# Weights' buffers at four places within 256 bytes, in a two-block sequence model on one core

## The reference

```python
h = rms_norm(x, norm_g)
parts = jnp.split(h @ w_in, split_idx, axis=-1)
...
return x + mixed @ w_out
```

## Time and profile before

| what | value |
|---|---|
| time, median of 3 runs | 3272.28 us (3271.72 to 3272.84) |
| the profiled execution | 3274.4 us |
| its span, first to last instruction | 3272.6 us |
| mean granted TensorE clock | 0.998 of 2.4 GHz |
| instructions | 43,047 |
| matmuls | 15,826, of them 12,672 in the units |

### The profile page before, as it was taken

The page is one execution under the profiler, slowest core; times in us unless marked ns, Lnnn a source line. Parts: engine busy times, 40 slices in busy tenths (PEclk is TensorE's granted clock), DMA queues, the critical chain, the costliest instruction groups (busy, mean ns, idle before and its releaser), DMA issues.

```text
span 3272.6 us, 43047 instructions
## 1 busy us (share of the span) xinstructions
PE 3250.9 (99%) x15826; PEld 2643.6 (81%) x15826; DVE 2089.6 (64%) x3172; ACT 1268.8 (39%) x1987; POOL 141.8 (4%) x116
## 2 busy tenths in 40 slices
PE   8999999999999999999999999999999999999999
PEld 7888888787888888888878887787778888778777
DVE  5665656687776566534264776677757477676863
ACT  4333324445443345523132224524534222642641
POOL 3000000001020000000020000000002000000000
PEclk9999999999999999999999999999999999999999
DMA  5333436677776676746453454545547354555445
GB/s 178 123 124 109 136 125 196 213 247 264 253 277 203 196 223 191 249 174 212 148 179 106 148 171 148 187 146 177 186 170 255 109 171 132 188 166 180 172 163 203
DMA packets 302097, 588.83 MB, mean 180 GB/s; under 512 B 64280, under 2 KB 111128, under 8 KB 301888
## 3 DMA queue, kind: packets, MB, share of 16 engines
q1 hardware_dynamic: 301888, 586.09, 53.7%
HBM read 453.77 MB, written 132.20 MB: 179 GB/s over the span
## 4 chain that ended last, share of the span: by engine, by line
PE 93%; DVE 3%; ACT 1%; DVEq 1%; DMA 1%; issue 1%; SPq 0%; ACTq 0%
PE bank L561 70%; PE bank L560 13%; PE bank L2007 1%; PE bank L1102 1%; PE bank L738 1%; PE bank L1132 1%; PE bank L1422 1%; PE bank L1453 1%; PE bank L1608 0%; PE bank L1597 0%; PE bank L2328 0%; DVEq L2638 0%; PE bank L1007 0%; PE bank L1610 0%; PE bank L2358 0%
## 5 line engine op out<-in xcount | busy, mean ns | idle before, releaser
L561 PE MATMUL bank<-act_high,weights_high 128*128 128x512 f32 x3584 | 1424.7, 398 | 14.7 <-DVE act_low L544 11.3
L561 PE MATMUL bank<-act_low,weights_high 128*128 128x512 f32 x3584 | 1401.6, 391 | 0.0
L473 DVE TENSOR_TENSOR weights_low<-weights_raw,weights_high 128x1024 fp32r<-128x1024 f32 x528 | 654.4, 1240 | 724.5 <-ACT weights_high L404 711.2
L404 ACT ACTIVATE weights_high<-weights_raw 128x1024 fp32r<-128x1024 f32 x528 | 557.5, 1057 | 1416.3 <-PE bank L561 1206.8
L561 PE MATMUL bank<-act_high,weights_low 128*128 128x512 f32 x3584 | 963.0, 389 | 0.0
L561 PEld LDWEIGHTS bank<-act_high,weights_high 128*128 128x128 f32 x3584 | 676.1, 189 | 163.8 <-DVE act_low L544 11.3
L561 PEld LDWEIGHTS bank<-act_low,weights_high 128*128 128x128 f32 x3584 | 676.2, 189 | 136.2 <-issue 1.2
L561 PEld LDWEIGHTS bank<-act_high,weights_low 128*128 128x128 f32 x3584 | 672.7, 188 | 140.1
L560 PE MATMUL bank<-weights_high,act_high 128*128 128x512 f32 x640 | 253.1, 396 | 0.0
L560 PE MATMUL bank<-weights_high,act_low 128*128 128x512 f32 x640 | 249.4, 390 | 0.0
L2105 DVE SCALAR_TENSOR_TENSOR residual_in<-residual_in,arena 128x512 f32<-128x512 f32 x240 | 181.2, 755 | 20.3 <-issue 1.5
(11 more groups left out here) (323 smaller groups left out, 2484.2 us busy)
## 6 DMA issues: line engine op xcount, KB each, us to landing
weights_raw<-in_w_all SPq DMA_DIRECT2D x528, 512.0 KB, 3.5
convert_in<-mix SPq DMA_DIRECT2D x80, 256.0 KB, 4.4
fm_b<-stream_out SPq DMA_DIRECT2D x72, 256.0 KB, 3.3
mix<-arena SPq DMA_DIRECT2D x64, 256.0 KB, 3.1
x_part<-stream_out SPq DMA_DIRECT2D x48, 256.0 KB, 4.4
residual_in<-x_part SPq DMA_DIRECT2D x48, 256.0 KB, 5.4
x<-stream_out SPq DMA_DIRECT2D x48, 256.0 KB, 5.2
convert_in<-x SPq DMA_DIRECT2D x48, 256.0 KB, 4.0
```

Of the source, the lines that this page charges most:

```text
L404: e.activation(WH[:, t % 3, :], RAW[:, t % 3, :], ACT.Copy).then_inc(wh_ready, 1)
L473: e.tensor_tensor(WL[:, t % 3, :], RAW[:, t % 3, :], WH[:, t % 3, :].bitcast(F32), ALU.subtract).then_inc(wl_ready, 1)
L561: return e.matmul(bank[s][:, :], a[:, s * P:(s + 1) * P], h, start=start, stop=stop)
```

## The change

The three positions of weights_high and weights_low are cut from tensors that have 64 columns more, at columns 16, 1056 and 2096, and 0, 1040 and 2080. In bytes, within 256 and counted from the activations' place, the positions of weights_high lie at 64, 128 and 192, those of weights_low at 0, 64 and 128. The arena gets 128 columns less, and everything declared between weights_low and the arena's end moves by 512 bytes, weights_low itself by 256.

```diff
-        WH = sb("weights_high", [P, 3, 2 * L], F32R)
-        WL = sb("weights_low", [P, 3, 2 * L], F32R)
+        WH_ALL = sb("weights_high", [P, 6 * L + 64], F32R)
+        WL_ALL = sb("weights_low", [P, 6 * L + 64], F32R)
+        WH = [WH_ALL[:, at:at + 2 * L] for at in (16, 1056, 2096)]
+        WL = [WL_ALL[:, at:at + 2 * L] for at in (0, 1040, 2080)]
...
-        ARENA_N = 20032
+        ARENA_N = 19904
...
-            e.activation(WH[:, t % 3, :], RAW[:, t % 3, :], ACT.Copy).then_inc(wh_ready, 1)
+            e.activation(WH[t % 3], RAW[:, t % 3, :], ACT.Copy).then_inc(wh_ready, 1)
...
-            e.tensor_tensor(WL[:, t % 3, :], RAW[:, t % 3, :], WH[:, t % 3, :].bitcast(F32), ALU.subtract
+            e.tensor_tensor(WL[t % 3], RAW[:, t % 3, :], WH[t % 3].bitcast(F32), ALU.subtract
                             ).then_inc(wl_ready, 1)
...
-                a = (WL if part == 2 else WH)[:, b, k * L:(k + 1) * L]
+                a = (WL if part == 2 else WH)[b][:, k * L:(k + 1) * L]
```

## The result

The changed kernel takes 3327.63 us in the median (3326.27 to 3328.73, 5 runs) against 3272.28 for the kernel before: a ratio of 1.0169, with a 95% interval of 1.0158 to 1.0180. It is slower by 55 us. The range of the prediction (3215 to 3360) holds it. The forecast itself, no change, did not come; the loss that the first rival priced did, in a milder form than its full price.

A forecast was written before the change was run, and what follows sets the result against it. TensorE's matmul spacing was taken to bound the kernel. Writers, shifted memory, displaced products and settling were each taken as 0, sum 0, so the forecast stayed at 3272.3 us, range 3215 to 3360.

The forecast's parts named there:

- Rival 1: Displaced products lose their rhythm as load and stream pieces meet: 7.7 ns each, +87 us, 3359 us; slower had chance 0.34.
- line 738's price: Upper price per displaced product, from line 738's 234.4 ns against 226.7: 7.7 ns, x 11,264 = +87 us.
- What bounds the kernel: TensorE, busy 3250.9 of 3272.6 us; the start-to-start spacing of 12,672 matmuls, 226.7 ns each, makes 88% of the span.
- the extra 13.3 ns: Time per matmul over the 213.3 ns of 512 columns at 2.4 GHz; 169 us in all, which buffer places could change.
- the small group that has 7.7 more: Line 738: 32 matmuls of the same shape, stationary operand displaced by 96 bytes, 234.4 ns each instead of 226.7.
- the settling: Matmul runs settle into 226.7 ns; settling anew in each unit was priced at most 28 us, taken as 0.
- Writers, slices, moved tensors, 512 bytes: ScalarE and VectorE writing displaced buffers, and the 512-byte shift of what follows in memory, each cost 0.
- The products: 11,264 products with displaced weights in lines 561 and 560: between -150 and +87 us, taken as 0.
- The reading of line 738: Its operand, displaced by one and a half 64-byte pieces, cuts a ninth piece per load and finds no steady rhythm.
- Its case of 3326 us: Products displaced by 64 and 192 bytes lose the rhythm, those by 128 keep it: +54 us.
- Rival 2: Loads of displaced weights no longer meet the stream: -75 us for one piece, -150 for both; faster had chance 0.22.
- The rule of the Trainium skill: Loading the next weights takes no SBUF read bandwidth from the running matmul, so place means nothing and time is 3272 us.

The follow-up runs named there:

- run 1: Changed kernel, but all positions of both weight parts back at the activations' place within 256 bytes, one period on; 3272.30 us, ratio 1.0003.
- run 3: Kernel before, with padding so that only small_weights, line 738's operand, moves to the activations' place within 256 bytes; 3272.18 us.
- run 4: Changed kernel, with each position's low part at its high part's place (64, 128, 192 bytes past the activations'); 3322.88 us, ratio 1.0155.
- run 5: Changed kernel, with both parts of all positions at 192 bytes past the activations' place; 3300.71 us, ratio 1.0090.
- run 9: Kernel before, places unchanged, each matmul of the units split into two of 256 columns with a weight load each; 3421.34 us.
- run 10: Changed kernel with its four places, each matmul of the units split into two of 256 columns with a load each; 3352.09 us.
- run 11: Against the kernel before: all weights at 64 bytes past the activations' place, 256-column halves only where weights are stationary; 3301.60 us, ratio 1.0086.
- run 12: Against the kernel before: stationary weights at 64 bytes with 256-column halves, moving weights whole at place 0; 3293.07 us, ratio 1.0068.

## Why the prediction was right, and where it failed

The range held because it took in line 738's price; the forecast at its centre missed by 55 us, where the prediction had said that 6.5 us can be told.

- **What bounds the kernel**: right. The extra 13.3 ns, the small group that has 7.7 more, and the settling were the rows that mattered, and line 738 was shown to be a matter of place.
- **Writers, slices, moved tensors, 512 bytes**: right; run 1 prices them all together at nothing, 1.0003.
- **The products**: this is the step that failed. "I take 0" rested on 64 bytes being the unit, with 96 bad only because it is no multiple of 64. The measured spacing at 64, 128 and 192 is 233.2, 232.4 and 229.1 ns; the period is 256 bytes as far as tried (run 1), and of the thirteen places only 0 runs at 226.7 throughout, and that where all weights lie there. Of the two known rows, line 738's was the nearer one after all.
- **The reading of line 738** that carried this step was wrong as well, and the trace of the kernel before had the answer. It was said not to settle in 32 matmuls. Its first start is at 64.55 us; from there, every seventh is:

```profile
66.19 0.39 PE L738 MATMUL bank<-act_low,small_weights 128*128 128x512 f32 x1
...
67.83 0.39 PE L738 MATMUL bank<-act_high,small_weights 128*128 128x512 f32 x1
...
69.47 0.39 PE L738 MATMUL bank<-act_low,small_weights 128*128 128x512 f32 x1
...
71.11 0.39 PE L738 MATMUL bank<-act_high,small_weights 128*128 128x512 f32 x1
```

They are 1.64 us apart, four times over. The group is settled, in a longer cycle: 238, 237, 231, 234, 235, 234, 231 ns, the same to 1 ns in all three groups, and 1.64 us are 246 pieces of 6.67 ns. The commonest cycles at the other places tried here are whole numbers of pieces too: 34 in one step at 0, 35 at 64 (or 70 in two), 103 in three at 192, 244 in seven at 128; with halves, 18 in one at 0 and 17 in one or 53 in three at 64. So that a rhythm counts in whole pieces does not tell a good place from a bad one.

- **Rival 1** has the sign and the order of what happened; its mechanism, pieces that meet, no run shows. Its price per displaced product, 7.7 ns, was an upper bound as named: the mean over all products rose by 4.8 ns, from +3 at 192 to +6 at 64 with stationary weights. Its case of 3326 us, with 128 keeping the rhythm, came to the measured time by way of two errors that cancel, a 128 that loses 5 and places that lose less than 7.7.
- **Rival 2**: no place gains with 512 columns. With 256 columns 64 does gain a piece against 0, so the idea was not empty, only not for this kernel.
- **Settling** per unit was kept at up to 28 us. It is there (230.4 ns in the low part that stayed at 0), worth 1408 x 3.7 = 5 us. What was not foreseen is that a change of place can also put all the products of the next part into a worse cycle, as the 37 high parts at 192 show.
- **The rule of the Trainium skill** (TensorE: Matmul & The Clock Gate, Step-by-step: what each phase is for) that loading the next tile's weights steals no read bandwidth from the running matmul does not cover what these fp32r operands show: the spacing depends on where the two operands lie to each other (runs 1, 3, 4 and 5), and at place 0 one more load and matmul per 512 columns cost 13.3 ns more (run 9). Whether read bandwidth is what is lost, no run shows. The N / 2.4 GHz + 2.5 ns of the Trainium skill (same page, section Wait — 56ns, not 53.3ns?) was not reached at any place or length by the matmuls of the units: 226.7 ns against its 215.7 at 512 columns, and 120.0 and 113.3 against 109.2 at 256, an estimate by that page.

Open: what in the chip meets. That the load and the stream read the same SBUF in pieces, and that one of them gives way, is contradicted by none of the twelve runs, but it was only argued. No run took the loads away, and no model of it foretold runs 10 to 12 or says which cycle a place gets.

## What to carry to other kernels

Where back-to-back matmuls bound a kernel, read the distance between their starts, and compare groups of the same shape: a few ns per matmul that no wait explains can be the place of one operand to the other within 256 bytes. In fp32r with 512 columns keep stationary and moving operand at the same place; in this kernel it is worth 1.7% against the four places tried, and a single small tensor in between (96 bytes) is enough to push the next ones off. If the columns per load change, measure the places anew, and in a run that has interruptions like the real one.

## What the runs showed of the hardware that I had not expected

The step between matmuls is a cycle of fixed numbers that repeats to about a nanosecond, seven long at 128 and at 96, three at 192, and its sum is a whole number of 6.67 ns, the time of 16 columns. The same operands at the same places can run in two lasting rhythms, 113.3 and 117.8 ns at 64 with halves, and what came before decides which. And twice the weight loads can be free: two halves at 64 in the good rhythm take 226.7 ns, exactly what one whole matmul takes at place 0.
